# The head of a two-layer diffusion step: sums, modulation rows and first products in another order

## The reference

```python
mod = silu(c) @ w_ada[l] + b_ada[l]            # 6 x 1024 per stream: shift, scale, gate, shift, scale, gate
h = x * rsqrt(mean(x*x) + 1e-6) * norm_mix_g   # rmsnorm over the 1024 channels of a token
h = h * (1 + scale) + shift
q, k, v, u_rwkv, u_fnet = split(h @ w_in)      # one projection, 2176 columns
```

## Time and profile before

| | us |
|---|---|
| three runs | 1796.02, 1796.92, 1797.6 (median 1796.92) |
| the profiled execution | 1801.61 |
| its span | 1799.8 |
| TensorE busy | 1722.3 (96%) |
| VectorE, ScalarE, GpSimd busy | 1034.1, 808.6, 386.8 |

### The profile page before, as it was taken

The page is one execution under the profiler, slowest core; times in us unless marked ns, Lnnn a source line. Parts: engine busy times, 40 slices in busy tenths (PEclk is TensorE's granted clock), DMA queues, the critical chain, the costliest instruction groups (busy, mean ns, idle before and its releaser), DMA issues.

```text
span 1799.8 us, 45769 instructions
## 1 busy us (share of the span) xinstructions
PE 1722.3 (96%) x19531; PEld 1622.0 (90%) x19531; DVE 1034.1 (57%) x2258; ACT 808.6 (45%) x1715; POOL 386.8 (21%) x318
## 2 busy tenths in 40 slices
PE   7999998899999999999999999888999999999997
PEld 5999776779899999999989987777899999999997
DVE  4445666663583673738453556765629648365663
ACT  4433655552453452525453357464335425344352
POOL 2344010223303002020434521002260110201113
PEclk9999999999999999999999999998999999999999
DMA  9755301005613223231345270200032232323311
GB/s 329 227 141 161 99 5 49 6 14 146 174 41 101 71 71 94 68 109 53 100 141 129 82 202 4 47 6 6 26 111 72 76 95 60 105 62 92 85 57 59
DMA packets 215972, 161.09 MB, mean 90 GB/s; under 512 B 21968, under 2 KB 213146, under 8 KB 215770
## 3 DMA queue, kind: packets, MB, share of 16 engines
q1 hardware_dynamic: 213818, 156.13, 29.6%
q0 software_dynamic: 1952, 2.03, 0.4%
HBM read 154.99 MB, written 3.15 MB: 88 GB/s over the span
## 4 chain that ended last, share of the span: by engine, by line
PE 85%; DVE 7%; ACT 4%; issue 2%; SPq 1%; DMA 1%; POOL 0%; ACTq 0%; DVEq 0%; POOLq 0%
PE PS L1155 27%; PE PS L1118 19%; PE PS L1119 19%; PE PS L1078 2%; PE PS L1417 2%; PE PS L1379 2%; PE PS L1402 1%; PE PS L1012 1%; DVE mix L2663 1%; ACT mix L2039 1%; DMA mix<-in_w_in 1%; SPq L788 1%; PE PS L1616 1%; PE PS L1660 1%; PE PS L996 1%
## 5 line engine op out<-in xcount | busy, mean ns | idle before, releaser
L2816 DVE SCALAR_TENSOR_TENSOR x<-PS,mod,x 128x320 f32<-128x320 f32 (+2 forms) x240 | 90.8, 433 | 283.6 <-PE PS L1119 283.6
L848 POOL TENSOR_TENSOR SfR<-ring,SfR 128x768 fp32r<-128x768 f32 (+1 forms) x24 | 41.1, 1714 | 627.2 <-ACT SfR L1884 627.2
L1155 PE MATMUL PS<-T_hi,wsplit 128*128 128x320 f32 x768 | 170.0, 309 | 0.0
L1118 PE MATMUL PS<-in_hi,win 128*128 128x320 f32 x480 | 149.8, 320 | 1.5 <-ACT mix L1913 1.5
L1119 PE MATMUL PS<-in_hi,win 128*128 128x320 f32 x480 | 144.6, 309 | 0.0
L1118 PE MATMUL PS<-hid_hi,wsplit 128*128 128x320 f32 x440 | 132.9, 310 | 0.0
L1119 PE MATMUL PS<-hid_hi,wsplit 128*128 128x320 f32 x440 | 132.5, 309 | 0.0
L1155 PEld LDWEIGHTS PS<-T_hi,wsplit 128*128 128x128 f32 x768 | 128.3, 188 | 0.0
L1155 PE MATMUL PS<-h_hi,wsplit 128*128 128x320 f32 x576 | 127.6, 309 | 0.0
L1155 PE MATMUL PS<-T_lo,wsplit 128*128 128x320 f32 x384 | 118.7, 309 | 0.0
L2207 ACT ACTIVATE wsplit<-Sf 128x512 fp32r<-128x512 f32 x96 | 59.8, 629 | 127.8 <-DVE Sf L2866 70.1
(11 more groups left out here) (555 smaller groups left out, 5378.1 us busy)
## 6 DMA issues: line engine op xcount, KB each, us to landing
ring<-in_w_ada SPq DMA_DIRECT2D x47, 1024.0 KB, 7.8
ring<-in_ffn_w_in SPq DMA_DIRECT2D x88, 512.0 KB, 5.2
ring<-in_ffn_w_out SPq DMA_DIRECT2D x16, 768.0 KB, 4.4
ring<-in_ffn_w_out SPq DMA_DIRECT2D x16, 640.0 KB, 4.1
ring<-in_w_in SPq DMA_DIRECT2D x7, 1024.0 KB, 9.0
ring<-in_w_in SPq DMA_DIRECT2D x10, 512.0 KB, 5.8
ring<-in_w_in SPq DMA_DIRECT2D x16, 256.0 KB, 5.4
ring<-in_w_out SPq DMA_DIRECT2D x16, 256.0 KB, 6.0
```

Source lines behind the costliest of these rows:

```text
L848: nc.gpsimd.tensor_tensor(lo, raw_w, hi, SUB).then_inc(wl_ready(), 1)
L1118: mm(lat[:, 0:TH], w, v[:, 0:TH], start=(n == 0), stop=(n == total - 1))
L1155: last = mm(bank[:, 0:TH], (w_lo if p == 1 else w_hi)[:, k, :], (v_lo if p == 2 else v_hi)[:, k, :], start=(q in (A11, A12, S1_) and k == ...
L2816: last = V.scalar_tensor_tensor(x[:, m, a:b], bank[:, at:at + b - a], mod[:, gate_at + m, s:s + 1], x[:, m, a:b], MUL, ADD)
```

## The change

It reorders the head of layer 0 on four engines. SyncE issues `side(0)` ahead of chunk 2 instead of behind chunk 3. TensorE does all eight sums first, then the parameter transpose, row 0, the broadcast, columns 0, the warming matmuls, pass 0 of tiles 0 and 1, row 1, pass 1 of tiles 0 and 1, columns 1, row 2. ScalarE loads the table of the square root ahead of its first square, by a small activation of its own. VectorE takes the reciprocal ahead of its work on row 0, and copies row 1 behind the scaling of the first four tiles.

```diff
@@ SyncE
             for n, (l, kind, i) in enumerate(CHUNKS):
+                if n == 2:
+                    side(0)
                 if n == SLOTS:
-                    side(0)
                     side(1)
@@ TensorE
-                    for k in range(2):
+                    for k in range(KT):
                         head_part(k)
                     small()
                     ada_rows(0, l)
-                    for k in range(2, KT):
-                        head_part(k)
+                    inverse(0)
                     ada_cols(0, l)
-                    ada_rows(1, l)
-                    ada_cols(1, l)
-                    inverse(0)
...
-                    head_units((0, 1), (0, 1))
+                    head_units((0, 1), (0,))
+                    ada_rows(1, l)
+                    head_units((0, 1), (1,))
+                    e.wait_ge(h_scaled.sem, h_scaled.upto(l, 4))
+                    ada_cols(1, l)
                     ada_rows(2, l)
@@ ScalarE
                 if l == 0:
+                    load_root_table()
                     for k in range(0, KT, 2):
@@ VectorE, norm_apply
                 for k in range(4):
                     scale(k)
                 if l == 0 and which == 0:
+                    row_copy(1)
                     mod_part(l, 1, 1)
@@ VectorE, start of layer 0
+                    norm_inverse(l, 0)
                     row_copy(0)
...
                     mod_part(l, 0, 1)
-                    norm_inverse(l, 0)
-                    row_copy(1)
                     norm_apply(l, 0)
```

## The result

The kernel after takes 1803.84 us (median of 15 runs, 1799.22 to 1808.01), the kernel before 1797.46 (15 runs, 1794.8 to 1802.16). The ratio is 1.0033, with a 95% interval of 1.0025 to 1.0042: slower by 5.9 us, between 4.5 and 7.5 (the two medians themselves lie 6.4 apart). The direction is the one forecast, and the size is off: +3.7 was forecast. On the base that the forecast added to (1796.92) the ratio gives 1802.9, inside the range (1796.0 to 1803.6); the median of the timed executions lies 0.2 above its upper end.

The account below looks back on a forecast made before the run. TensorE's unbroken work was taken as the bound, so E's shift was the kernel's: 3.7 from row 1's place plus S - 30.12, +3.8 rounded to 3.7, on 1796.92 gives 1800.6 us, range 1796.0 to 1803.6.

Parts of the forecast that it names:

- What bounds the kernel: TensorE, 85% of the chain, unbroken from 34.38 us; the head pays only by shifting when that work begins.
- E: End of the high-pass products of tiles 2 and 3, where column product 2 starts; 40.65 before, its shift the kernel's.
- The stall at tile 2: Row 1 between the first products delays modulation part 1; TensorE idles 1.45 ahead of tile 2; loss 3.7 us.
- T1: When tile 1 of the input is ready: S + 3.98; 34.10 before, 34.2 forecast.
- S: Start of the first scaling of h; 30.12 us in the kernel before.
- Row 1's clock: Row 1 between the first products, priced at 1.89 us; column product 1 starts at T1 + 4.0.
- rival C: Lower clock lasts through row 1 and first products, or the table load waits; middle +5.5, 1802.4 us; chance 0.13.
- S = 30.2: First scaling, from early table load, sums in a row, row 0 at lower clock, broadcast to 29.1, then part 0's 1.1.
- Nothing for the side buffer and for row 1's weights: Side buffer lands near 22.3, cover 1.7; row 1's weights land near 28.3, wanted at 34.8; no cost.
- The seventh ring chunk: Issued at 37 behind row 1, lands between 40.0 and 48.9, needed near 45.7; taken as nothing, upper end 3.2.
- Rival D: Layer 1's low-clock stretch, 1213.75 to 1227.19, is in timed executions before and vanishes: -4.4, 1796.2 us; chance 0.13.

Follow-up runs that it names:

- e2: The kernel after with VectorE's copy of the parameters and `omka` ahead of the reciprocal; 1.0035 of the kernel before, +6.3 us.
- e3: The kernel after without the early load of the root table; 1.0030 of the kernel before, +5.4 us.
- e4: The kernel after with six warming products added ahead of the sums; 1.0034 of the kernel before, +6.1 us.
- e10: The kernel after with nine warming products instead of four ahead of the products; 1.0036 of the kernel before, +6.5 us.
- e11: The kernel after run once more, unedited; 1.0036 of the kernel before, +6.5 us.
- e5: The kernel before with row 1 alone moved between the products, its copy behind the fourth scaling; 1.0025 of the kernel before, +4.5 us.
- e7: The kernel after with ScalarE's, and so GpSimd's, weight splits held until the gain of part 0 is done; 1.0049 of the kernel before, +8.8 us.
- e1: The kernel after with row 1 back ahead of the warming products; 1.0018 of the kernel before, +3.2 us.
- e8: The kernel after with earlier table load, `omka`, first split and row 1, warming ahead of sums, columns 1 between tiles 0 and 1; 0.9999 of before, -0.2 us.
- e9: e8 with five warming products ahead of row 1 instead of four behind it; 1.0011 of the kernel before, +2.0 us.
- e6: The kernel before with the side buffer's transfer alone moved ahead of chunk 2; 1.0001 of the kernel before, +0.2 us.
- e12: The same edit as e6, run again; 1.0019 of the kernel before, +3.4 us.

## Why the prediction was right in direction and short in size

*What bounds the kernel.* Right in the main. The time follows E: in twelve of the thirteen rows of the table that have a ratio E's shift and the time lie within 2.8 us of each other, and behind E TensorE's 129.3 us without a break are the same in both kernels. It follows it roughly only: among after, e2, e3, e4, e10 and e11 E differs by 3.6 us and the time by 1.1.

*The stall at tile 2 (T1 + 10.25 - 6.55 = +3.7).* Right. T1 = S + 3.98 held (36.60 against 32.62). From column product 1 to E passed 6.34, forecast 6.25; idle ahead of tile 2 was 1.71, forecast 1.45. e5, the move by itself, gave +4.2 in E and +4.5 in time. (The forecast added +3.8 up and rounded it down to +3.7.)

*Row 1's clock: the step that failed first.* The forecast priced row 1 at 1.89 and column product 1 at T1 + 4.0. It came at T1 + 6.44. From T1 to row 1 passed 1.41 where 0.8 was taken for tile 1's four high matmuls and the switch (+0.6), row 1 took 3.64 (+1.75), and from its end to column product 1 passed 1.39 for 1.3 (+0.1). This is rival C, with its late load too, though only the first part of the products ran low, not pass 1; C had 0.13 and +5.5. The forecast read the clock at row 0 and then took it as full from the warming products on, though its own times left TensorE idle for about 1.0 us ahead of the first product and 1.3 ahead of tile 1; the late S made the first of these 3.04. e10 shows that the gap is the cause: with more warming products in it row 1 took 1.95.

*S = 30.2: the step that failed second; it was 32.62.* Four terms went into it. The load began behind VectorE's copy, at 16.78, not at ScalarE's own last copy: first square 18.18, +0.8 on the forecast 17.36, just inside the bound of +1.3. It was read from the earlier trace rows, where a load ran ahead of its activation's wait; here it did not run ahead of the wait for x. The sums (pairs of 1.61, forecast 1.64) and row 0 (3.19, forecast 3.4) were about as taken. Column product 0 came at 29.63, forecast 29.1. From it to the scaling passed 2.99, forecast 1.1: this is the hold of `omka`, and it was in no bound and no rival. With no split beside it (e7) 1.23 passed. The forecast had GpSimd's split ending at 30.6 and VectorE's work on part 0 at 29.1 to 30.2, one beside the other, and priced both as if alone. The sum for E is then 3.8 forecast + 2.4 at S + 2.4 at column product 1 + 0.1 = 8.7. So the forecast of the time was nearer than its account of the head: +3.7 stood against +8.7 in E and only +5.9 in time, and that E's shift did not arrive whole was no part of it. That is luck, and it holds for rival C's +5.5 as well, which did not have the hold.

The trace of before held the sign, unread. Timeline of the kernel before, the gain of part 0 and that of part 1:

```profile
27.03 0.16 DVE L2320 SCALAR_TENSOR_TENSOR gain<-mod,par 128x4 f32<-128x4 f32 x1
...
33.43 0.82 DVE L2320 SCALAR_TENSOR_TENSOR gain<-mod,par 128x4 f32<-128x4 f32 x1
```

The same instruction took 0.16 with GpSimd idle and 0.82 beside its second split, ending at 34.25 where the split ends at 34.24. The Trainium skill, "SBUF — State Buffer", section "SBUF: two separate sides", has the rule: VectorE and GpSimd share a pair of ports under an exclusive lock, and a VectorE operation with two SBUF inputs or in a 2-port mode that comes second waits for GpSimd's whole instruction. The traces agree: the gain reads `mod` and `par` from SBUF and was held in before, e1, e2, e3, e4, e8 and e9 (0.46 to 1.88 for 0.16), while the copies out of PSUM at 29.03 and 29.24 of after took 0.29 and 0.26 beside the splits, as they do with GpSimd idle. `omka` has one input, `par`, and was held too (2.32 for 0.17); in which mode it runs no trace shows. The reciprocal, from SBUF as well, began inside the first split in e8 and e9 and took its usual 1.15, so not every operation from SBUF is held.

*Nothing for the side buffer and for row 1's weights.* Right for this kernel, wrong as a part by itself: +2.6 in E in e6 and e12. The cover was the later place of row 1, which the forecast named. *The seventh ring chunk, nothing*: right, TensorE waits for no transfer from 49 to 75 us.

*Rival D.* The profiled execution before held the stretch of the earlier trace rows and that of after did not, which is 4.8 us between two single executions. The ratio over 15 executions of each is still +5.9, so D did not happen in the time. e5 held the same stretch, so it is not the kernel before alone that can. How often timed executions hold such a stretch is open.

*What stays open.* The head of after is 8.7 and 9.1 later, the time 5.9 and 6.5 longer; some 2.5 us of it do not arrive. The traces show no work behind the head that gives them back: without its low-clock stretch the profiled execution before would be near 1796.8, and that of after is 1805.29, 8.5 apart. That leaves the scatter of such stretches, or heads of the timed executions that differ from the profiled ones, and nothing here tells the two apart. e2, e3, e4 and e10 show a gain of 2.5 to 3.2 in E over after and none in the time; of these e4 and e10 held a low stretch in their profiled executions, e2 and e3 did not. Whether a shift of the head brings such a stretch or whether it comes by chance was not settled.

## What to carry to other kernels

When a small operation is put on the path, look at what the engine that shares ports with it does in the same microseconds; its price is then the rest of the neighbour's instruction, not its own 0.17 us. When dense TensorE work is put behind a gap, price it at both levels of the clock, not only the first work behind the gap. And when a transfer is moved ahead, ask which work it pushes back, even if the new order happens to cover it.

## What the runs showed of the hardware that was not expected

- An operation of VectorE on 128x2 elements took 2.32, 1.93 and 1.86 us (after, e11, e10) instead of 0.17, ending with GpSimd's instruction.
- The narrow sums did not bring the clock back: from 20 to 25 us of the kernel after TensorE was busy for 4.27 of 5.00 and the granted clock was 0.50 (windows of the kernel after: busy of PE, PEld, DVE, ACT, POOL, then clock, DMA share, GB/s):

```profile
20.00:25.00 5.00, 4.27 (x56) 1.21 (x48) 2.48 (x3) 2.08 (x3) 0.00 (x0) 0.50 1.10 349
```

- The load of a table began behind the wait of the work ahead of it in one place (16.78, 0.15 behind VectorE's copy) and ahead of a wait in another.
- Executions differ by several us behind the head, where the kernels do the same work: the time for 2805 matmuls in layer 1 was 153.8, 149.0 and 147.5 us in three profiled executions (before, after, e9), the longest of them with the 13.44 us at the lower level of the earlier trace rows. Two executions of one program (e6, e12) took 1752.5 and 1754.9 us from E to the end.
